# The first output projection of a two-layer mixer: two of its four weight pieces begun before the last transposes instead of one

## The reference

```python
def merge_groups(att, h_ml, o_pre, g_att, g_ml, w_out):
    B, T = att.shape[:2]
    att_n = rmsnorm(att, g_att)
    hf = h_ml.astype(jnp.float32)
    hn = hf * lax.rsqrt(jnp.mean(hf * hf, axis=-1, keepdims=True) + EPS)
    hn = hn * g_ml.astype(jnp.float32).reshape(ML_HEADS, ML_V_DIM)
    ml = hn.reshape(B, T, ML_WIDTH).astype(att.dtype) * jax.nn.sigmoid(o_pre)
    return jnp.concatenate([att_n, ml], axis=-1) @ w_out
```

## Time and profile before

| | |
|---|---|
| median of 3 runs | 2428.91 us |
| lowest, highest | 2428.79, 2431.15 us |
| the profiled execution | 2426.68 us |
| its span in the trace | 2424.9 us |
| PE busy (matmuls), share of the span | 2361.8 us, 97% |
| DVE, ACT, POOL busy | 1685.4, 1234.9, 422.1 us |
| PE's share of the chain that ended last | 91% |
| mean granted clock of PE | 0.983 |

### The profile page before, as it was taken

One profiled execution on the slowest core, in us unless ns is written; L12 is line 12 of the kernel. 1 busy time (PEld: TensorE's weight loads), 2 busy tenths in 40 slices (PEclk: granted clock), 3 DMA queues, 4 the chain that ended last, 5 costly groups with the idle time before them and its releaser, 6 DMA issues.

```text
span 2424.9 us, 34897 instructions
## 1 busy us (share of the span) xinstructions
PE 2361.8 (97%) x13364; PEld 1976.9 (82%) x13364; DVE 1685.4 (70%) x1977; ACT 1234.9 (51%) x1473; POOL 422.1 (17%) x353
## 2 busy tenths in 40 slices
PE   9999999999999998899999999899999999999998
PEld 7669998769998876778888887688888888888887
DVE  6556774566864567577655358658888888888887
ACT  6454343544333445431212145547777777777775
POOL 0002540002530000010002500003122231221222
PEclk9999999999998999999999999999999999999999
DMA  6574553514552320135555323029999989989995
GB/s 243 209 261 161 180 187 121 181 53 157 186 197 83 122 96 19 47 127 203 196 193 189 139 96 121 11 95 364 354 353 355 372 332 362 369 336 370 355 360 205
DMA packets 73253, 506.76 MB, mean 209 GB/s; under 512 B 8696, under 2 KB 9336, under 8 KB 13440
## 3 DMA queue, kind: packets, MB, share of 16 engines
q1 hardware_dynamic: 70704, 496.68, 55.7%
q0 software_dynamic: 2384, 7.84, 1.1%
HBM read 503.41 MB, written 1.08 MB: 208 GB/s over the span
## 4 chain that ended last, share of the span: by engine, by line
PE 91%; DVE 5%; ACT 2%; issue 1%; DMA 0%; DVEq 0%; SPq 0%; ACTq 0%
PE ps L479 87%; PE ps L544 1%; PE ps L1301 1%; DVE ring_r L2283 1%; PE ps L827 1%; DVE h L2257 0%; ACT ring_hi L1612 0%; DVE temp L2348 0%; DVE h L2868 0%; DMA ring<-in_stream 0%; ACT h L1661 0%; PE ps L676 0%; DVE h_r L2248 0%; PE ps L587 0%; ACT h L2063 0%
## 5 line engine op out<-in xcount | busy, mean ns | idle before, releaser
L1612 ACT ACTIVATE ring_hi<-ring 128x2048 fp32r<-128x2048 f32 (+1 forms) x429 | 807.5, 1884 | 551.1 <-PE ps L479 332.0
L3061 DVE TENSOR_TENSOR ring_r<-ring,ring_hi 128x2048 fp32r<-128x2048 f32 x264 | 614.5, 2337 | 110.4 <-ACT ring_hi L1612 107.1
L2283 DVE TENSOR_TENSOR ring_r<-ring,ring_hi 128x2048 fp32r<-128x2048 f32 (+2 forms) x165 | 377.6, 2295 | 170.7 <-ACT ring_hi L1612 157.0
L479 PE MATMUL ps<-extra_r,ring_hi 128*128 128x256 f32 (+1 forms) x1432 | 459.4, 321 | 1.3 <-DVE h_r L2251 1.2
L479 PE MATMUL ps<-extra_r,ring_r 128*128 128x256 f32 (+1 forms) x1432 | 456.4, 319 | 0.0
L479 PE MATMUL ps<-h_r,ring_hi 128*128 128x256 f32 (+2 forms) x1400 | 443.7, 317 | 0.0
L479 PE MATMUL ps<-ring_hi,extra_r 128*128 128x512 f32 (+2 forms) x1104 | 427.6, 387 | 5.1 <-DVE ring_r L2283 4.0
L479 PE MATMUL ps<-ring_hi,areaA_r 128*128 128x512 f32 x1056 | 418.3, 396 | 0.3 <-DVE ring_r L3061 0.3
L479 PE MATMUL ps<-ring_r,areaA_r 128*128 128x512 f32 x1056 | 413.3, 391 | 0.0
L479 PEld LDWEIGHTS ps<-extra_r,ring_hi 128*128 128x128 f32 x1432 | 272.5, 190 | 24.0 <-DVE h_r L2251 4.0
L479 PEld LDWEIGHTS ps<-extra_r,ring_r 128*128 128x128 f32 x1432 | 272.2, 190 | 18.9
(11 more groups left out here) (375 smaller groups left out, 2987.8 us busy)
## 6 DMA issues: line engine op xcount, KB each, us to landing
ring<-in_experts SPq DMA_DIRECT2D x264, 1024.0 KB, 4.9
ring<-in_stream SPq DMA_DIRECT2D x200, 1024.0 KB, 4.9
ring<-in_stream SPq DMA_DIRECT2D x10, 512.0 KB, 3.6
areaB<-mrow_out POOLq DMA_DIRECT2D x24, 128.0 KB, 3.2
ring<-in_stream SPq DMA_DIRECT2D x2, 576.0 KB, 4.0
res<-in_xT SPq DMA_DIRECT2D x2, 512.0 KB, 4.1
res<-in_ctxT POOLq DMA_DIRECT2D x1, 1024.0 KB, 7.4
h<-in_consts POOLq DMA_DIRECT2D x2, 512.0 KB, 5.3
```

What stands on the lines that cost most here:

```text
L479: return pe.matmul(o, l, r, start=start, stop=stop, skip_group_check=True)
L1612: return act.activation(dst, src, ACT.Copy)
L2283: L.send(TTN(ring_lo[:, s, 0:n], ring[:, s, 0:n], ring_hi[:, j % HIS, 0:n].bitcast(F32), ALU.subtract), "weights_lo")
L3061: TTN(ring_lo[:, s, :], ring[:, s, :], ring_hi[:, j % HIS, :].bitcast(F32), ALU.subtract).then_inc(sig("weights_lo"), 1)
```

## The change

`out_begin` now begins two pieces, 0 and 1, on feature tiles 0 to 3: piece 0 in banks 4 and 5 as before, piece 1 in banks 6 and 7, which the last two steps of the matrix memory have used. `out_end` ends both, feature tile by feature tile, and releases both chunks with the last sum (bank 7). `out_project` does only pieces 2 and 3. The first sums of squares, which stood behind piece 1, go behind piece 2, where now steps 0 to 3 stand in a row. The bank turn is set on by 4 instead of 2: piece 2 now uses banks 0 and 1 (before 1 and 2), the sums of squares bank 2 (before 0), and piece 3 banks 3 and 4 as before, as does all that follows.

```diff
--- before.py
+++ after.py
@@ -616,31 +616,35 @@
             def out_begin(tag, w, n):
 
                 first_split[tag] = len(splits)
-                v = split_chunk(Piece(*w, 0, D, 0, 256), "p (k c) -> p k c", k=8)
-                us = [take(tag, m2, bank=4 + m2) for m2 in range(2)]
-                for k in range(4):
-                    pe.wait_ge(sig("mixT_ready"), n - 7 + k)
-                    for m2 in range(2):
-                        mm3(ps[:, us[m2].bank, :], lambda s: v[s][:, k, m2 * P:(m2 + 1) * P],
-                            lambda s: att_lo[:, k, 0:2 * T] if s else h_hi[:, 0:2, k, :], k == 0, False)
-                return v, us
-
-            def out_end(v, us, n):
+                begun = []
+                for c in range(2):
+                    v = split_chunk(Piece(*w, 0, D, c * 256, (c + 1) * 256), "p (k c) -> p k c", k=8)
+                    us = [take(tag, 2 * c + m2, bank=4 + 2 * c + m2) for m2 in range(2)]
+                    begun.append((v, us))
+                    for k in range(4):
+                        pe.wait_ge(sig("mixT_ready"), n - 7 + k)
+                        for m2 in range(2):
+                            mm3(ps[:, us[m2].bank, :], lambda s: v[s][:, k, m2 * P:(m2 + 1) * P],
+                                lambda s: att_lo[:, k, 0:2 * T] if s else h_hi[:, 0:2, k, :], k == 0, False)
+                return begun
+
+            def out_end(begun, n):
 
                 for k in range(4, KD):
                     pe.wait_ge(sig("mixT_ready"), n - 7 + k)
-                    for m2 in range(2):
-                        m = mm3(ps[:, us[m2].bank, :], lambda s: v[s][:, k, m2 * P:(m2 + 1) * P],
-                                lambda s: hs[s][:, 0:2, k, :], False, k == KD - 1)
-                        if k == KD - 1:
-                            full(m, us[m2])
-                release_with(us[1])
+                    for v, us in begun:
+                        for m2 in range(2):
+                            m = mm3(ps[:, us[m2].bank, :], lambda s: v[s][:, k, m2 * P:(m2 + 1) * P],
+                                    lambda s: hs[s][:, 0:2, k, :], False, k == KD - 1)
+                            if k == KD - 1:
+                                full(m, us[m2])
+                release_with(begun[-1][1][1], 2)
 
             def out_project(tag, w, halves, n, norm, pairs=False, early=False):
 
                 if not early:
                     first_split[tag] = len(splits)
-                for c in range(1 if early else 0, 4):
+                for c in range(2 if early else 0, 4):
                     v = split_chunk(Piece(*w, 0, D, c * 256, (c + 1) * 256), "p (k c) -> p k c", k=8)
                     for m2 in range(2):
                         u = take(tag, 2 * c + m2)
@@ -662,7 +666,7 @@
                         full(m, u)
                     release_with(u)
                     if c in (1, 2):
-                        sum_squares(norm, (c - 1) * halves, c * halves)
+                        sum_squares(norm, 0 if early else (c - 1) * halves, c * halves)
 
             def transpose_mix(l, f, tiles, bank=None):
 
@@ -1231,8 +1235,8 @@
                 for f in range(4 if l == 0 else 0, 8):
                     transpose_mix(l, f, mixed)
                 if l == 0:
-                    out_end(*begun, 16)
-                    turn[0] += 2
+                    out_end(begun, 16)
+                    turn[0] += 4
                 out_project(f"out{l}", ("w_out_2", l), 2 if l == 0 else 1, 16 + 8 * l, f"n2_{l}", early=l == 0)
                 sum_squares(f"n2_{l}", 4 if l == 0 else 2)
                 if l == 0:
```

## The result

The changed kernel takes 2435.01 us, the median of 9 runs (2431.2 to 2440.72); the kernel before took 2429.43 beside it (2426.74 to 2432.54, 9 runs). The ratio is 1.0025 [1.0016, 1.0033]: slower by 6 us (5.6 between the medians). The forecast was 2429.2, in 2426.2 to 2431.8, with 92% for no change. The profiled execution took 2431.20 us, 4.5 more than that of before.

A forecast was written before the change was run, and what follows sets the result against it. PE was taken to bound the kernel, busy 2361.8 of 2424.9 us. Terms 0 + 0 + 0 + 0.25 on the median 2428.91 gave 2429.2 us, range 2426.2 to 2431.8, with 92% for no change.

The forecast's parts named there:

- The sums of squares: Four steps in a row behind piece 2 instead of two groups of two: 3.81 us against 3.56, so +0.25 us.
- The stated bound of +1.2: Upper bound for the joined steps behind piece 2, with both squares of 0.63 us wholly uncovered; lower bound -0.08.
- The clock as a rival: PE's clock falls in the moved transpose gap: briefly, +0.8 us, 2430.0 (8%), or for 26 matmuls or more (4%).
- the long case: Low clock for 26 or more matmuls behind the gap; all 48 would give +9.3 us, 2438.4; chance 4%.
- A granted clock of 0.50 behind 1003: Sign of a wrong forecast in the profile after: PE at half clock behind the gap, whose end was forecast at 1003.37.
- theory A2: From the experiments: how long the clock stays low behind joined steps depends on when it last rose.
- The moved half: 24 matmuls of piece 1 go from behind the transpose gap to before it: 5.44 us moved, sum 0.
- the ending feature by feature: Behind the gap, the remaining 48 matmuls of pieces 0 and 1 run on four banks in turn: cost 0.
- the later splits and loads: Weight splits for pieces 2 and 3, and loads into the slots of pieces 0 and 1, stay covered: cost 0.
- The gap: From the transposes of tiles 4 and 5 to piece 0's rest: stays 4.85 us, 2.75 idle, merely later.
- the idle times go: Rival: the 24 moved matmuls cover PE's waits for tiles 6 and 7, -2.75 us, 2426.4 us; chance 9%.
- The rule on transposes: Skill rule that transposes do not count as busy alike, so the transpose-only gap could cost the clock; rows showed no fall.

## Why the prediction was wrong

*The sums of squares: the step that failed.* It forecast 3.73 + 0.08 us for four steps in place of 3.56, +0.25, from the earlier trace rows. The measured term: steps and piece 3 take 17.74, 17.74, 17.74 and 17.75 us in the four traces after, for 2 x 1.70 + 10.97 = 14.37 before: +3.4. The pattern of waits was taken over rightly; ACT's squares are where they were forecast. What it left out is that the four steps in the earlier trace rows cost the clock too: in the trace before it fell at 1043.0. There the norm follows, and the fall cost 1.1 us of the tail, unseen since it stood in the trace already. Moved in front of piece 3, four steps have 48 dense matmuls behind them, and the same four steps behind piece 3 are still there. The row gave the duration of the group, and not what the group does to its successor. The stated bound of +1.2 was for waits alone.

*The clock as a rival.* It was tied to the moved gap only, and given 8% for a brief fall (+0.8 us) and 4% for a long one. In the gap it came as the brief one: a fall in every trace that has two begun pieces ahead of an unfilled gap (6 of 6), against 1 of 4 with one. How the gap lies to the clock's last rise may decide, which was not tested. Read from windows of 0.25 us, the gap with one piece began 4.5, 4.6 and 4.8 us behind that rise in the traces without a fall, and 4.9 in the one with it; with two pieces it began 10.2 to 10.5 us behind. Its price from the transposes to the sums of squares was 1.0 us in five of the six, near the 0.8 forecast, and 2.7 in the sixth (six dense matmuls between the steps), where the clock stayed low twice as long. The single fall with one begun piece cost 1.6. For the long case the prediction counted 48 matmuls behind the gap; the changed kernel has 96. "A granted clock of 0.50 behind 1003" was named as a sign of error, and came. That the sparse steps could do the same was not among the rivals.

*The two together.* Filling the gap takes away 1.0 us there and 1.6 in the steps and piece 3; parting the steps then takes away another 16.15 - 14.37 = 1.8. Of these 4.4 us the profiled execution got 1.1 back in the tail and 0.3 in the 48 matmuls ahead of the gap (11.49 for 6.35 + 5.44), which leaves its 2.9. Where PE met the low clock in the gap, the steps' clock fell 2.8 us in and stayed low for 6.8 us (4 of 4 traces). Where it didn't, the fall came about 4 us in and lasted 3.4 us (3 of 3). The kernel with piece 1 inside the gap and joined steps came out as theory A2 expected (0.9994 and 12.6 us or less, against 0.9995 and 12.60), which speaks for its view that the second fall's length hangs on when the clock last changed. In the four traces of the changed kernel the second fall comes 27.3 us behind the first each time. Why the first fall moves the second is not shown.

*The moved half, the ending feature by feature, the later splits and loads: 0.* Right. With both falls removed the stretch is 61.91 us against 61.91. The banks and weights were waited for nowhere: the trace after has no idle time at 994.29 (piece 1), 1016.61 (piece 2) or 1031.74 (piece 3).

*The gap: 4.85 us, unchanged.* Nearly right: 5.20, with the idle times ended by DVE's scaling as said; the 0.35 is the last transposes at low clock. The rival "the idle times go" was rightly rejected for this place of the work, and the version with piece 1 inside the gap shows what its 2.75 us need: the stretch shrinks by 2.9.

*The rule on transposes.* In the gap, PE had only 16 transposes for 5 us, and the clock fell in 6 of 6 traces. The Trainium skill, "TensorE: Matmul & The Clock Gate" (section on PE-mode transpose), says that they do not count as busy in the same way. The falls fit this, but do not show it: some 2.4 of the 5.2 us were plain idle time, and no run here has transposes without idle time for as long. The prediction gave the rival too little weight because one trace of before showed no fall. Four traces with one begun piece show three without and one with a fall: one trace does not tell what a gap does to the clock.

*What stays open.* The stretches after are longer by 2.9, 5.1, 2.8 and 3.0 us than 61.91, and the three of before differ from it by 0, 0.6 and 0.03: some 3.2 us on average. The ratios say 6, 6 and 9 us (5.6, 5.4 and 7.6 between the medians). In these traces the rest of the program does not show the missing 3 us. From the network's first matmul to the end of the span it takes 1376.26, 1378.39 and 1377.16 us before, and 1376.35, 1381.01, 1379.20 and 1374.82 after. The means lie 0.6 us apart, while one kernel's traces differ by up to 6.2, mostly around 1421 and 1576 to 1633. That scatter is too wide to exclude a loss of 3 us in seven traces. Whether one sits there all the same, or three of the four profiled executions were by chance among the faster ones (2431.20, 2432.0 and 2430.75, but 2436.13, against medians of 2435 to 2437), was not settled.

*The version to keep.* Two pieces begun, the second between the transposes of tiles 5 and 6, and the steps two by two: 0.9987 and 0.9994 of the kernel before, the second not clear of 1. No other version was better; with the steps joined it can't be told from this one.

## What to carry to other kernels

When small operations are gathered or moved, look at the granted clock behind the place they come from, and ask what will stand behind them at the new place: here 3.4 us of low clock cost 1.1 us ahead of the norm with its waits and 1.6 in the dense piece 3, and 6.8 us there cost 2.5. Put sparse work in short runs between dense work, or work into the idle time itself, behind the instruction that starts the loop and not ahead of it. Where the clock can change, one trace shows a possible course, so take several before trusting an absence.

## What the hardware showed

- One-column matmuls in a row can drop the clock although PE and its weight loads read busy 1.00. With 32 in a row (3.5 to 4.3 us) ahead of piece 3 it fell in all seven traces that have them, in four inside the row and in three just behind it. Behind piece 3 the row of 32 stands in 15 traces: it fell inside the row in seven, in three only in the norm's small matmuls behind it, and not at all in five. What decides is not shown. In the four traces of the changed kernel that row began 8.1 to 8.2 us behind the clock's last rise, and the clock fell in one of them and held in three. With 16 in a row (1.70 us) it never fell; nor with 16, six dense matmuls and 16 more.
- Dense bf16 matmuls in idle time went with a clock of 1.00 through a gap of 4.85 us in two kernels, one trace each; the gap did not grow by a hundredth. Both gaps also began a little nearer behind the last rise (9.8 and 10.0 us) than the six that lost the clock (10.2 to 10.5), so two traces do not quite exclude chance.
- While the clock is low, dense work pays about 0.2 us more per matmul of 512 columns: 0.43 from start to start for 0.2266. In piece 3, 12 such matmuls make the 2.5 us.
- Executions of one kernel on one chip spread over 10 us (2424.3 to 2434.51 in 35 runs of the kernel before), with the clock's falls at other places in each trace.
